# Two channel tiles of a depthwise convolution: diagonal products and tap sums replaced by chunk products of four tokens by 32 channels

## What is computed

```python
def conformer_conv(g, dw_w, dw_b, ln_g, ln_b):
    u = g[..., :CONV_CHANNELS] * jax.nn.sigmoid(g[..., CONV_CHANNELS:])
    y = lax.conv_general_dilated(
        u, dw_w[:, None, :].astype(u.dtype), window_strides=(1,),
        padding=[(CONV_WIDTH - 1, 0)], dimension_numbers=('NWC', 'WIO', 'NWC'),
        feature_group_count=CONV_CHANNELS) + dw_b
    return jax.nn.silu(layernorm(y, ln_g, ln_b))
```

## Time and profile before

| what | us |
|---|---|
| median of three runs | 3022.51 (3020.09 to 3024.55) |
| the profiled execution | 3030.46 |
| its span, first to last instruction | 3028.7 |
| PE busy in the span | 2924.4 (97%) |
| DVE busy | 1714.8 (57%) |
| ACT busy | 1061.6 (35%) |
| POOL busy | 213.1 (7%) |
| stage e, first product to the last before the common output code | 1749.3 to 2000.5 |

### The profile page before, as it was taken

The page is one execution under the profiler, slowest core; times in us unless marked ns, Lnnn a source line. Parts: engine busy times, 40 slices in busy tenths (PEclk is TensorE's granted clock), DMA queues, the critical chain, the costliest instruction groups (busy, mean ns, idle before and its releaser), DMA issues.

```text
span 3028.7 us, 38678 instructions
## 1 busy us (share of the span) xinstructions
PE 2924.4 (97%) x14206; PEld 2413.4 (80%) x14206; DVE 1714.8 (57%) x2639; ACT 1061.6 (35%) x1601; POOL 213.1 (7%) x256
## 2 busy tenths in 40 slices
PE   7999999999999999999999999989999988999998
PEld 6888888888888778878888876588888875788887
DVE  5555535765576666654455576646444576464445
ACT  4332323443344332224332323434232345442222
POOL 1000000000000000001000000015502110110001
PEclk9999999999999999999999999989999999999999
DMA  4322232122221233332232331013333310223332
GB/s 146 97 96 85 92 104 77 56 63 77 78 62 56 63 105 95 95 97 90 90 97 83 97 102 45 29 55 106 92 95 96 99 63 16 62 85 96 96 97 90
DMA packets 70400, 252.14 MB, mean 83 GB/s; under 512 B 7808, under 2 KB 9856, under 8 KB 69632
## 3 DMA queue, kind: packets, MB, share of 16 engines
q1 hardware_dynamic: 68112, 241.89, 25.9%
q10 hardware_dynamic: 2016, 7.96, 0.7%
q0 software_dynamic: 144, 0.52, 0.0%
HBM read 248.25 MB, written 2.10 MB: 83 GB/s over the span
## 4 chain that ended last, share of the span: by engine, by line
PE 84%; DVE 8%; ACT 4%; issue 3%; POOL 1%; DMA 0%; DVEq 0%; ACTq 0%; POOLq 0%
PE ps L297 17%; PE ps L299 17%; PE ps L298 17%; PE ps L568 2%; PE ps L569 2%; PE ps L570 2%; ACT w_high L277 2%; DVE w_low L284 2%; PE ps L779 1%; PE ps L780 1%; PE ps L781 1%; PE ps L1803 1%; PE ps L853 1%; PE ps L591 1%; PE ps L839 1%
## 5 line engine op out<-in xcount | busy, mean ns | idle before, releaser
L284 DVE TENSOR_TENSOR w_low<-raw,w_high 128x1024 fp32r<-128x1024 f32 x456 | 565.8, 1246 | 420.8 <-ACT w_high L277 413.7
L297 PE MATMUL ps<-h_high,w_high 128*128 128x512 f32 x1872 | 737.8, 394 | 6.4 <-DVE arena L1464 3.0
L299 PE MATMUL ps<-h_high,w_low 128*128 128x512 f32 x1872 | 729.9, 390 | 0.0
L298 PE MATMUL ps<-h_low,w_high 128*128 128x512 f32 x1872 | 729.4, 390 | 0.0
L277 ACT ACTIVATE w_high<-raw 128x1024 fp32r<-128x1024 f32 x456 | 477.9, 1051 | 450.9 <-PE ps L299 204.0
L297 PEld LDWEIGHTS ps<-h_high,w_high 128*128 128x128 f32 x1872 | 352.3, 188 | 78.3 <-DVE arena L1464 3.4
L299 PEld LDWEIGHTS ps<-h_high,w_low 128*128 128x128 f32 x1872 | 351.8, 188 | 73.9
L298 PEld LDWEIGHTS ps<-h_low,w_high 128*128 128x128 f32 x1872 | 352.3, 188 | 70.1
L297 PE MATMUL ps<-y_high,w_high 128*128 128x512 f32 x640 | 250.4, 391 | 0.6 <-DVE y_low L1938 0.3
L298 PE MATMUL ps<-y_low,w_high 128*128 128x512 f32 x640 | 249.1, 389 | 0.0
L299 PE MATMUL ps<-y_high,w_low 128*128 128x512 f32 x640 | 249.0, 389 | 0.0
(11 more groups left out here) (443 smaller groups left out, 4526.0 us busy)
## 6 DMA issues: line engine op xcount, KB each, us to landing
raw<-stream SPq DMA_DIRECT2D x456, 512.0 KB, 3.6
table<-tables_in ACTq DMA_DIRECT2D x5, 1088.0 KB, 6.5
x<-x_in ACTq DMA_DIRECT2D x8, 256.0 KB, 8.3
x_out<-x SPq DMA_DIRECT2D x16, 128.0 KB, 1.7
const<-const_in SPq DMA_DIRECT2D x1, 673.0 KB, 7.9
arena<-ssm_in POOLq DMA_DIRECT2D x1, 512.0 KB, 5.8
params<-params_in ACTq DMA_DIRECT2D x1, 287.0 KB, 6.7
```

The lines of the kernel that those rows point to most:

```text
L284: nc.vector.tensor_tensor(w_low[:, u.slot], raw[:, u.raw], w_high[:, u.slot].bitcast(F32), ALU.subtract).then_inc(weights_low, 1)
L297: nc.tensor.matmul(bank, wh, high[:, k], start=k == 0, stop=False)
L298: nc.tensor.matmul(bank, wh, low[:, k], start=False, stop=False)
L299: mm = nc.tensor.matmul(bank, wl, high[:, k], start=False, stop=k == tiles - 1)
```

## The change

For the tiles 2 and 3 the convolution is made in another layout. A tile is cut into four quads of 32 channels, and time into 128 chunks of 4 tokens. On the 128 rows now stand 4 tokens by 32 channels of a quad, and along a row the chunks, with 8 chunks of zeros ahead. An output chunk depends on itself and the 8 chunks before it, so nine 128 x 128 matrices per quad, with the taps on shifted diagonals, do the 31 taps: 36 products of 128 columns for a tile, in the slots 26 to 28 (tile 2) and 34 to 36 (tile 3).

- **PE**: the 41 diagonal products (line 1803) go; 72 products of 128 x 128 by 128 columns come.
- **POOL**: makes the 72 matrices, four in one operation of 128 x 512 from a mask and a table of taps, 18 operations; the first four in slot 18. There are four areas for them; two are in `work`, two are in the unused accumulators of the tiles 2 and 3.
- **ACT**: the 41 scaled identities and one copy with bias go; two copies of a bank of PSUM come (slots 28 and 36).
- **DVE**: the 21 taps of tile 3 and the two joins go. The gates of the tiles 2 and 3 become 16 operations each of 32 x 128, which read every fourth token and write to the rows of the new layout. The way back, with the bias, is 16 operations a tile of 32 x 128, which write every fourth token (four in each of the slots 30 to 33 and 37 to 40). At the start of the stage, after the wait for the tables and ahead of the lambda sums, stand two more clears, three operations for the mask, and 32 copies of 32 rows that build the table of taps and the bias.

The tables of slots:

```diff
+        E_BATCH, E_AREAS = 4, 4
+        E_FILTER = {26: (2, 0, 12), 27: (2, 12, 24), 28: (2, 24, 36), 34: (3, 0, 12), 35: (3, 12, 24), 36: (3, 24, 36)}
+        E_EVICT_SLOT = (28, 36)
+        E_SPREAD_SLOT = {**{30 + q: (2, q) for q in range(4)}, **{37 + q: (3, q) for q in range(4)}}
+        E_BUILD = {18: range(0, 4), 26: (4, 5), 27: (6, 7), 28: (8,), 29: (9, 10), 33: (11,), 34: (12, 13), 35: (14, 15),
+                   36: (16, 17)}
```

On PE:

```diff
+                    if n0 == 0:
+                        pe.wait_ge(e_gated, 2 + 16 * (tile + 1))
+                        pe.wait_ge(e_exp, (6, 14)[tile])
+                    for n in range(n0, n1):
+                        q, k = divmod(n, E_BACK + 1)
+                        batch = E_BATCHES * tile + n // E_BATCH
+                        if n % E_BATCH == 0:
+                            pe.wait_ge(e_built, batch + 1)
+                        at = n % E_BATCH * P
+                        mm = nc.tensor.matmul(ps[:, 2, q * P:(q + 1) * P], e_area[batch % E_AREAS][:, at:at + P],
+                                              e_stack[tile][:, q, k:k + E_CHUNKS], start=k == 0, stop=k == E_BACK)
+                        if n % E_BATCH == E_BATCH - 1:
+                            mm.then_inc(e_filtered, 1)
```

On ACT:

```diff
-                        nc.scalar.activation(e_diag[:, n % E_RING], ident, ACT.Copy,
-                                             scale=par("dw_w", 31 * m + j)).then_inc(e_tapped, 1)
+                    act.wait_ge(e_filtered, E_BATCHES * (tile + 1))
+                    nc.scalar.activation(e_acc[:, E_STACKED[tile]], ps[:, 2], ACT.Copy).then_inc(e_joined, 1)
```

On DVE at the start of the stage:

```diff
-            nc.vector.memset(e_u[:, :, 0:PADT], 0.0)
+            nc.vector.memset(e_u[:, 0:2, 0:PADT], 0.0)
+            nc.vector.memset(e_stack[0][:, :, 0:E_BACK], 0.0)
+            nc.vector.memset(e_tap_w, 0.0).then_inc(e_ready, 1)
...
+            for q in range(E_QUADS):
+                rows = slice(32 * q, 32 * q + 32)
+                for i in range(E_CHUNK):
+                    to = slice(32 * i, 32 * i + 32)
+                    nc.vector.tensor_copy(e_tap_w[to, :, q, 5 - i:5 - i + CONV_WIDTH], taps[rows]).then_inc(e_ready, 1)
+                    nc.vector.tensor_copy(e_bias[to, 2 * q:2 * q + 2], par("dw_b", 2, 2)[rows]).then_inc(e_ready, 1)
```

On DVE, the gate of the tiles 2 and 3:

```diff
+                            sg = e_sg[m % 2][rows].rearrange("p (c i) -> p i c", i=E_CHUNK)
+                            u = e_u[rows, m, PADT:].rearrange("p (c i) -> p i c", i=E_CHUNK)
+                            for i in range(E_CHUNK):
+                                nc.vector.scalar_tensor_tensor(out=e_stack[tile][32 * i:32 * i + 32, q, E_BACK:], in0=sg[:, i],
+                                                               scalar=1.0, in1=u[:, i], op0=ALU.add,
+                                                               op1=ALU.mult).then_inc(e_gated, 1)
```

On DVE, the way back:

```diff
+                    dve.wait_ge(e_joined, tile + 1)
+                    y = e_conv(m)[32 * q:32 * q + 32].rearrange("p (c i) -> p i c", i=E_CHUNK)
+                    for i in range(E_CHUNK):
+                        rows = slice(32 * i, 32 * i + 32)
+                        nc.vector.tensor_scalar(y[:, E_CHUNK - 1 - i], e_acc[rows, m, q * P:(q + 1) * P],
+                                                e_bias[rows, 2 * q + tile:2 * q + tile + 1], None,
+                                                op0=ALU.add).then_inc(e_tap, 1)
```

On POOL:

```diff
+                        pool.wait_ge(e_ready, 4 + 2 * E_QUADS * E_CHUNK)
+                        if batch >= E_AREAS:
+                            pool.wait_ge(e_filtered, batch - E_AREAS + 1)
+                        if tile == 1 and batch % E_AREAS == 3:
+                            pool.wait_ge(e_tap, E_TAPPED + 16)
+                        nc.gpsimd.tensor_tensor(e_area[batch % E_AREAS].rearrange("p (e h) -> p e h", e=per),
+                                                e_mask.unsqueeze(1).to_broadcast(shape), taps.unsqueeze(2).to_broadcast(shape),
+                                                ALU.mult).then_inc(e_built, 1)
```

112 lines of the change are left out of this document (52 added, 60 removed).

## The result

The changed kernel takes 3042.86 us (median of 4 runs, 3040.39 to 3044.94), the kernel before 3023.09 in the same comparison: a ratio of 1.0066, with a 95% interval of 1.0049 to 1.0084. The change costs 15 to 25 us; the prediction was 3040, slower. The profiled execution took 3043.9 us, where the prediction's sum for such an execution was 3048.3.

The account below looks back on a forecast made before the run. PE is busy 97% of the span, but its saving was expected to be lost to waits, mainly for DVE's small operations. Terms 9.3 + 3.5 - 1 + 7 - 1 = +17.8 us gave 3040 on the median, range 3026 to 3052.

Parts of the forecast that it names:

- PE's own work: On PE, 41 diagonal products of 35.3 us become 72 new ones of 16.0; alone it would gain 19 us.
- The unit price: On DVE, a 32-row gate operation takes 0.38 us, its step 0.41; sixteen are 6.6 us, 16 of the way back 6.4.
- A: Start of the stage: copies, clears and mask ahead of the lambda sums delay PE whole, plus slow clock; +9.3 us.
- sign of being wrong: The prediction said it is wrong if, among other signs, the copies at the start are 0.1 us apart.
- The slow clock: At the start, PE runs at the lower clock for a while after its long stall; put at 1.5 us.
- B: Slot 18: POOL's first four batches hold DVE just before PE waits for it; +3.5 us.
- C: Slots 24 to 28: removed diagonal products and ACT work against the gate, a longer stall and POOL waiting; -1 us.
- D: Slots 29 to 36: way back and gate on DVE delay mix 7 and PE's transposes; +7 us.
- E: Slots 37 to 44: 8.6 us of diagonal products leave, but PE waits there anyway, so the end barely moves; -1 us.
- PE's busy time: Sign in the profile after: PE's busy time falls by 15 to 19 us while the span grows.
- that rival: DVE's small operations follow every 0.13 us, so PE's saving counts: -8.7 us, 3014; chance 0.08.
- the heavier rival: POOL binds as well, its batches late for PE and holding DVE's gate and way back: +27 us, 3049.5; chance 0.13.

Follow-up runs that it names:

- x1: Changed kernel, with DVE building mask, table of taps and bias before the wait for the stage's tables: 3036.03 us, ratio 1.0040 to the kernel before.
- x6: Changed kernel with x5's edit, the filter's 36 products in two slots per tile instead of three, and POOL's batches moved to match: 3037.07 us, ratio 1.0050.
- x8: Kernel before, with 36 of its 41 diagonal products cut to 16 columns, nothing added: stage 232.6 us, 18.9 shorter.
- x7: Kernel before, with 8 of tile 3's 10 diagonal products cut to 16 columns: stage 247.3 us, 4.2 shorter.
- x2: Changed kernel, with POOL's first four batches moved behind slot 20's rotation product and waiting for slot 21's soft: stage 267.9 us, 0.9 shorter.
- x3: Changed kernel, with each of POOL's 18 batches cut from 128 x 512 to 128 x 16: stage 265.2 us, 3.6 shorter.
- x5: Changed kernel, with DVE's mix ahead of the gate in slots 25 and 33: stage 268.6 us, 0.2 shorter.
- x4: Changed kernel, with POOL's batch 11 also waiting for the mix of step 7: stage 267.0 us, 1.8 shorter.
- x11: Changed kernel, with gate operations reading 128 elements in a row instead of every fourth: stage 266.9 us, 1.9 shorter.

## Why the prediction was right, and where its parts were not

The forecast was 3040 and slower, the median is 3042.86: +19.8 over the kernel before, where +17.8 was forecast. What was to bind did bind: DVE's many small operations, ahead of what PE waits for, cost more than PE's saved work was worth (x1, x6, x8). That the total agrees to 0.1 us in the pair of profiles (17.7 against 17.8) is luck: the parts missed by up to 2.5 us each and cancelled, and the profile of the kernel before is itself, by the estimate above, at least 2.4 us too long in the stage.

- **PE's own work** was read rightly: a filter product is 0.222 us at full clock (sixteen instructions, eight products, span 1.95 us with the last one's tail), so twelve take 2.7; behind a stall sixteen take 3.62. That the saving would be covered was right in slots 41 to 43 (x7). For the rest x8 shows it real: the change lost because of what it added, not because PE had nothing to gain.
- **The unit price.** "So a gate operation is 0.38, its step 0.41": 0.379 and 0.409. The way back came to 0.33 a piece and 0.36 a step, not 0.384 and 0.40, a little less than in the row it was taken from, which reads PSUM and writes strided; which of the two makes the difference is not shown.
- **A, +9.3, measured +6.8.** The mechanism was right (x1), the size of one term off: 32 copies at 0.25 and 0.19 a step were to take 7.0 us; they took 4.7, since a pair has a step of 0.29 with durations of 0.18 and 0.15. The rule "step is duration plus 0.03", from long operations, does not hold for short ones; the starts are 0.11 and 0.18 apart in turn, so the prediction's own sign of being wrong, copies 0.1 apart, came for every second one. PE's wait for the norm column so came to 5.5 and not to about 8. The slow clock cost 1.4, as put (1.5); in x2, x3, x5 and x6, with the same program up to slot 18, it cost 2.7 to 2.8.
- **B, +3.5, measured +1.4.** Batches hold DVE, as said, but not all four stand ahead of what PE waits for. DVE comes to slot 18 as late as PE, 6.8 us. Its low part of a unit takes 2.31 us there in both kernels, beside the rotation's product. Only the two taps behind it, beside the first two batches, are longer, 2.98 us against 1.53, and then comes the product of the rotation for which PE waits. What batches 2 and 3 stretch (0.82 for 0.69, 2.32 for 1.53) stands behind it.

```profile
1811.86 2.98 DVE L2013 SCALAR_TENSOR_TENSOR arena<-arena,params 128x512 f32<-128x512 f32 x2
1814.77 0.68 DVE L2028 TENSOR_TENSOR ssq<-ps,table 128x512 f32<-128x512 f32 x1
```

```profile
1810.82 3.48 POOL L2134 TENSOR_TENSOR work<-const 128x512 f32<-128x512 f32 x2
```

- **C, -1, measured +0.8.** PE's transposes came 1.5 us earlier in their stretch, not 2.5: the gate took 7.47 instead of 6.6, since one of its operations stands beside the rotation's product of slot 26 and takes 1.34 us. That is the term of B in a place that the prediction did not look at. Behind the transposes 2.3 were added where 1.6 was put; the same stretch differs by 1.4 us between profiles of the same programs, so that part says little.
- **D, +7, measured +9.2.** "Mix 7 goes ... to 1904.3": with the earlier delay of 9.0 taken off it ended 9.1 later, not 8.3. DVE's chain alone was 7.3, less than forecast, because of the cheaper way back; 1.75 are batch 11 and the rotation's product beside the mix (x4). The prediction knew that POOL holds DVE and that batch 11 is in slot 33, and did not ask what sets it free. Behind it slots 34 to 36 added 2.5 where the prediction's -2.3, +2 and +1.5 make 1.2; the waits for POOL were 1.8 us there (1.51 and 0.29).
- **E, -1, measured -0.5**, confirmed by x7: slots 37 to 44 take 40.0 us in the kernel before, in x7 and in x8, and 39.6 in the changed kernel.
- **PE's busy time** fell by 12 us in all and by 9.5 in the stage, not by 15 to 19. The stage's granted clock went from 0.93 to 0.88, and the same products are busy for longer at the lower level, as the eight instructions of slot 3 are, 2.08 us instead of 1.16.
- **The rivals.** The small operations do not overlap at 0.13 us: the gate's step is 0.41; on the copies at the start that rival was partly right. POOL binds too, as the heavier rival has it, but for 3.6 to 5.5 us in all (x3); the forecast has a part of that in B and D, and the 9 us that this rival adds to it did not come.
- **The stride.** The Trainium skill, page "SBUF — State Buffer", section "Door 1: The DMA port swizzle", has fp32 up to four apart for free, from which the prediction made 0.29 us for a gate operation, as an estimate. That is what x11 measures without the stride (0.283); with it the operation takes 0.379. So reading every fourth element was not free here; the page's other statement, that two hits in a line are needed for full rate, agrees with that.
